# Expert loop of a mixture-of-experts encoder: token rows as the stationary operand, gate and up weights moving as high and low halves

## The reference, cut to what matters

```python
for e in range(N_EXPERTS):            # 32
    y = (jax.nn.silu(t @ e_gate[e]) * (t @ e_up[e])) @ e_down[e]
    out = out + combine[:, e:e + 1] * y
```

## Time and profile before

| | us |
|---|---|
| median of three runs (lowest, highest) | 893.04 (891.31, 894.35) |
| the profiled execution | 892.98 |
| its span | 891.0 |
| expert loop on PE, first transpose to last down matmul | 498.43 to 841.76 |

### The profile page before, as it was taken

The page is one execution under the profiler, slowest core; times in us unless marked ns, Lnnn a source line. Parts: engine busy times, 40 slices in busy tenths (PEclk is TensorE's granted clock), DMA queues, the critical chain, the costliest instruction groups (busy, mean ns, idle before and its releaser), DMA issues.

```text
span 891.0 us, 13079 instructions
## 1 busy us (share of the span) xinstructions
PE 771.9 (87%) x5022; PEld 641.3 (72%) x5022; DVE 373.1 (42%) x767; ACT 302.0 (34%) x539; POOL 329.7 (37%) x313
## 2 busy tenths in 40 slices
PE   3999999999977888999973599999999999999700
PEld 2788888866654554787873599999998899999600
DVE  5540000046768885412238233343333333333266
ACT  6211112145558887202220233333333333333222
POOL 2432256435556771501110123443433333442134
PEclk9999999979999999999995699999999999999955
DMA  8451112000010002426358189999999999996194
GB/s 273 108 151 48 47 48 71 1 0 1 2 48 0 1 1 76 137 69 219 113 172 300 38 258 335 351 349 351 348 349 350 347 342 347 350 352 231 40 370 195
DMA packets 111238, 160.21 MB, mean 180 GB/s; under 512 B 8304, under 2 KB 88656, under 8 KB 111072
## 3 DMA queue, kind: packets, MB, share of 16 engines
q1 hardware_dynamic: 104800, 142.78, 47.9%
q0 software_dynamic: 6400, 16.92, 5.9%
HBM read 144.99 MB, written 18.87 MB: 184 GB/s over the span
## 4 chain that ended last, share of the span: by engine, by line
PE 75%; DVE 9%; ACT 6%; DMA 4%; issue 3%; POOL 1%; SPq 1%; POOLq 0%; ACTq 0%; DVEq 0%
PE ps L768 26%; PE ps L583 6%; PE ps L585 6%; PE ps L584 6%; PE ps L788 3%; PE ps L787 3%; PE ps L792 3%; PE ps L623 3%; PE ps L759 2%; PE ps L648 2%; PE ps L707 2%; PE ps L709 2%; PE ps L708 2%; PE ps L664 2%; PE ps L670 2%
## 5 line engine op out<-in xcount | busy, mean ns | idle before, releaser
L768 PEld LDWEIGHTS ps<-xT,wg 128*128 128x128 f32 x1024 | 121.6, 195 | 5.9 <-ACT xT L1016 2.3
L768 PE MATMUL ps<-xT,wg 128*128 128x96 f32 x1024 | 121.4, 278 | 1.8 <-ACT xT L1016 1.8
L768 PE MATMUL ps<-xT,wu 128*128 128x96 f32 x1024 | 119.6, 275 | 0.0
L768 PEld LDWEIGHTS ps<-xT,wu 128*128 128x128 f32 x1024 | 116.9, 192 | 0.0
L1388 DVE TENSOR_TENSOR wdlo<-wd,wdhi 128x2048 fp32r<-128x2048 f32 x32 | 73.4, 2292 | 63.0 <-ACT wdhi L1036 63.0
L583 PE MATMUL ps<-hThi,whi 128*128 128x512 f32 x224 | 88.3, 394 | 4.2 <-DVE hTlo L1086 4.2
L585 PE MATMUL ps<-hThi,wlo 128*128 128x512 f32 x224 | 87.7, 392 | 0.0
L584 PE MATMUL ps<-hTlo,whi 128*128 128x512 f32 x224 | 87.7, 391 | 0.0
L1584 POOL COPY tokc<-tok 80x1 int32 (+1 forms) x32 | 54.1, 1689 | 42.7 <-DVE tok L1369 30.7
L1597 POOL COPY destc<-dest 80x1 int32 (+1 forms) x32 | 5.7, 178 | 166.7 <-DVE ysb L1380 166.7
L1536 POOL TENSOR_SCALAR pswa<-pswa,esum 128x384 f32<-128x384 f32 (+1 forms) x48 | 55.5, 1165 | 31.8 <-DVE esum L1173 31.4
(11 more groups left out here) (194 smaller groups left out, 1415.4 us busy)
## 6 DMA issues: line engine op xcount, KB each, us to landing
wg<-in_expert_w_gate SPq DMA_DIRECT2D x32, 1024.0 KB, 8.9
wu<-in_expert_w_up SPq DMA_DIRECT2D x32, 1024.0 KB, 12.7
wd<-in_expert_w_down SPq DMA_DIRECT2D x32, 1024.0 KB, 6.0
y<-expert_rows SPq DMA_DIRECT2D x16, 512.0 KB, 9.5
wraw<-in_w_in SPq DMA_DIRECT2D x14, 512.0 KB, 3.9
xin<-in_x SPq DMA_DIRECT2D x8, 512.0 KB, 5.6
xres<-in_x SPq DMA_DIRECT2D x16, 256.0 KB, 3.0
h_rows<-h SPq DMA_DIRECT2D x8, 512.0 KB, 2.7
```

The costliest lines, as they stand in the source:

```text
L768: mm = nc.tensor.matmul(ps[:, bank, f * COLS:(f + 1) * COLS], w[:, k, c0:c0 + P], xTu[:, k, :], start=(k == 0), stop=(k == KT - 1))
```

## The change

Gate and up are computed the way down already was. The gathered rows, transposed, are split into `xThi` and `xTlo` (80 columns, float32r) and are now the stationary operand. The gate and up weights move, 256 columns of gate and 256 of up side by side as 512, as a high part and a low part: 8 contraction pieces x 3 products = 24 matmuls of 512 columns per expert. The result has the tokens on the partitions, so the product `hx` (80x256) has to be transposed by PE (two pieces) before down.

The high parts live in `unit`, a ring of four 8 KB units per partition, three units per expert: two for the halves of gate and up, one for down. The low parts overwrite the loaded weights. ACT makes every high part (`half_high`, `down_high`), DVE every low part (`half_low`, `down_low`). The gate and up loads take 8 KB in one piece per partition ("(p k) f" in place of "(k p) f", with the h2 rows and the router weights permuted alike). The result rows leave PSUM in one ACT copy of 1024 columns. The index copies on POOL go. All loops over experts are written out in full.

The core of the diff:

```diff
+        unit = [at(f"unit{i}", [P, 2, 4 * DE], F32R, off) for i, off in enumerate((H + 56 * KB, H + 24 * KB, W + 56 * KB, V))]
+        def weight_unit(e, part):
+            return unit[(3 * e + (0, 1, 5)[part]) % 4]
+        def raw_half(w, e, a):
+            return w[e % RING][:, :, 4 * a:4 * a + 4, :].rearrange("p g k f -> p g (k f)")
 # SP
-                return (g_src.rearrange("(k p) f -> p k f", p=P), u_src.rearrange("(k p) f -> p k f", p=P),
+                return (g_src.rearrange("(p k) f -> p k f", p=P), u_src.rearrange("(p k) f -> p k f", p=P),
+                if e >= RING:
+                    sp.wait_ge(half_done, 2 * (e - RING) + 2)
...
+                if e >= RING:
+                    sp.wait_ge(down_done, e - RING + 1)
 # PE
+            def gate_up(e):
+                bank = ps[0:CAP, 2 + e % 2, :].rearrange("q (g f) -> q g f", g=2)
+                pe.wait_ge(xThi_done, e + 1)
...
+                for a in range(2):
+                    hi, lo = weight_unit(e, a), raw_half(wgulo, e, a)
+                    pe.wait_ge(ahi_done, 2 * e + a + 1)
+                    for k in range(4):   # xThi x hi
...
+                    for k in range(4):   # xTlo x hi
...
+                    pe.wait_ge(alo_done, 2 * e + a + 1)
+                    for k in range(4):   # xThi x lo
...
+                    mm.then_inc(half_done, 1)
+            def h_rows(e):
+                pe.wait_ge(h_made, e + 1)
+                for j in range(2):
+                    mm = nc.tensor.transpose(...)
+                mm.then_inc(htr_done, 1)
+            x_rows(0)
+            for e in range(N_EXP):
+                if e >= 1:
+                    h_rows(e - 1)
+                if e + 1 < N_EXP:
+                    x_rows(e + 1)
+                gate_up(e)
+                if e >= 1:
+                    down(e - 1)
+            h_rows(N_EXP - 1)
+            down(N_EXP - 1)
 # ACT
+            def half_high(e, a):
+                u = 3 * e + a
+                if a == 0:
+                    act.wait_ge(wgu_in[e % RING], 32 * (e // RING + 1))
+                if u >= 4:
+                    if a == 0:
+                        act.wait_ge(down_done, e - 1)
+                    else:
+                        act.wait_ge(half_done, 2 * (e - 1) + 1)
+                nc.scalar.copy(weight_unit(e, a)[:], raw_half(wgu, e, a)).then_inc(ahi_done, 1)
+            def down_high(e):
+                act.wait_ge(wd_in[e % RING], 16 * (e // RING + 1))
+                act.wait_ge(half_done, 2 * e + 2)
+                nc.scalar.copy(weight_unit(e, 2)[:], ...).then_inc(dhi_done, 1)
+            half_high(0, 0)            # ahead of the router's two Exp
...
+            half_high(0, 1)
+            x_high(0)
+            for e in range(N_EXP):
+                if e >= 1:
+                    h_high(e - 1)
+                if e + 1 < N_EXP:
+                    x_high(e + 1)
+                    half_high(e + 1, 0)
+                    half_high(e + 1, 1)
+                if e >= 2:
+                    rows_out(e - 2)
+                silu(e)
+                down_high(e)
 # DVE
+            for e in range(N_EXP):
+                if e >= 1:
+                    h_low(e - 1)
+                if e + 1 < N_EXP:
+                    x_low(e + 1)
+                    half_low(e + 1, 0)
+                    half_low(e + 1, 1)
+                gated(e)
+                down_low(e)
 # POOL: gather and scatter without the tokc and destc copies
-                gp.tensor_copy(tokc[u % 2][:], col).then_inc(idx_t, 1)
-                pool.wait_ge(idx_t, e + 1)
+                gp.indirect_dma_start(xg[e % 2][0:CAP, :], None, h2_d, bass.IndirectOffsetOnAxis(ap=tok[:, e:e + 1].bitcast(U32), axis=0),
```

More of the change, by code:

```diff
@@ L521, in _ @@
             sp.wait_ge(out_mm, 2 * TT)
[L522 to L526, removed]
+            for e in range(1, N_EXP):
+                fetch_expert(e)
             sp.dma_start(gbc[:], final_g.rearrange("(a d) -> a d", a=1).partition_broadcast(P)).then_inc(g_in, 16)
@@ L761, in ex_transposes, with x_rows @@
                 return mm
[L763 to L772, removed]
+            def x_rows(e):
+                pe.wait_ge(xg_in[e % 2], 16 * (e // 2 + 1))
+                if e >= 1:
+                    pe.wait_ge(xThi_done, e)
+                    pe.wait_ge(xTlo_done, e)
+                rows_transposed(xg[e % 2]).then_inc(etr_done, 1)
@@ L773, in down @@
                 for n in range(2):
                     for j in range(2):
-                        mm = nc.tensor.matmul(ps[0:CAP, b0 + n, :], hTu[:, j, 0:CAP], wd[u][:, j, n * 512:(n + 1) * 512],
-                                              start=(j == 0), stop=(j == 1))
-                return mm
[L779 to L788, removed]
+                        nc.tensor.matmul(ps[0:CAP, b0 + n, :], hThi_e[:, j, :], hi[:, j, n * 512:(n + 1) * 512], start=(j == 0), stop=False)
@@ L811, in down_of @@
[L811 to L823, removed]
+                        nc.tensor.matmul(ps[0:CAP, b0 + n, :], hTlo_e[:, j, :], hi[:, j, n * 512:(n + 1) * 512], start=False, stop=False)
@@ new lines, in down @@
+                    if n == 0:
+                        pe.wait_ge(dlo_done, e + 1)
+                    for j in range(2):
+                        mm = nc.tensor.matmul(ps[0:CAP, b0 + n, :], hThi_e[:, j, :], wdlo[e % RING][:, j, n * 512:(n + 1) * 512],
+                                              start=False, stop=(j == 1))
+                mm.then_inc(down_done, 1)
+            pe.wait_ge(hx_zero, 1)
+            x_rows(0)
[7 more added lines that the diff above has]
+                    down(e - 1)
@@ new lines, in _, with v_gate_up, v_down @@
+            h_rows(N_EXP - 1)
+            down(N_EXP - 1)
+            def v_gate_up(xTu):
+                for f in range(4):
+                    c0 = (f % 2) * P
+                    for k in range(KT):
+                        mm = nc.tensor.matmul(ps[:, 2, f * COLS:(f + 1) * COLS], wgu[0][:, f // 2, k, c0:c0 + P], xTu[:, k, :],
+                                              start=(k == 0), stop=(k == KT - 1))
+                return mm
+            def v_down(hTu):
+                for n in range(2):
+                    for j in range(2):
+                        mm = nc.tensor.matmul(ps[0:CAP, 4 + n, :], hTu[:, j, 0:CAP], wd[0][:, j, n * 512:(n + 1) * 512],
+                                              start=(j == 0), stop=(j == 1))
+                return mm
@@ L1013, in _ @@
             nc.scalar.activation(rs[:, 9, 0:TT], rs[:, 8, 0:TT], ACT.Exp).then_inc(r_exp, 1)
[L1015 to L1024, removed]
-                act.wait_ge(etr_done, e + 1)
-                if not first or u >= 2:
-                    act.wait_ge(gu_done, e - 1)
-                xT_copy(xT[u % 2]).then_inc(xT_done, 1)
-                if not first or u >= 2:
-                    y_low(it, u)
-                act.wait_ge(wd_in[u], it * 16 + 16)
-                if not first or u >= 2:
-                    act.wait_ge(down_done, e - 1)
-                elif u == 0:
-                    act.wait_ge(tok_done, 2)
-                nc.scalar.copy(wdhi[u % 2][:], wd[u][:]).then_inc(wdhi_done, 1)
-                act.wait_ge(gu_done, e + 1)
-                silu(sg[u % 2], 2 + u % 2).then_inc(silu_done, 1)
@@ L1040, in y_low @@
-            def y_low(it, u):
-                e = it * RING + u
-                par = u % 2
-                act.wait_ge(down_done, e - 1)
-                if not (isinstance(it, int) and it == 0):
-                    act.wait_ge(y_put[par], put_count(it, u - 2))
-                nc.scalar.copy(ysb[par][:, 0:512], ps[0:CAP, 4 + 2 * par, :]).then_inc(y_a, 1)
-            for u in range(RING):
-                expert(0, u)
-            with act.Fori(1, N_EXP // RING) as it:
-                for u in range(RING):
-                    expert(it, u)
@@ L1054, in _, with x_high, h_high @@
-            y_low(N_EXP // RING, 0)
-            y_low(N_EXP // RING, 1)
+            def x_high(e):
+                act.wait_ge(etr_done, e + 1)
+                if e >= 2:
+                    act.wait_ge(half_done, 2 * (e - 2) + 2)
+                nc.scalar.copy(xThi[e % 2][:].rearrange("p (b c) q -> p b c q", b=2),
+                               ps[:, 0:2, 0:4 * COLS].rearrange("p b (c q) -> p b c q", c=4)[:, :, :, 0:CAP]).then_inc(xThi_done, 1)
+            def h_high(e):
+                act.wait_ge(htr_done, e + 1)
+                if e >= 1:
+                    act.wait_ge(down_done, e)
+                nc.scalar.copy(hThi_e[:], ps[:, 2 + e % 2, 0:2 * COLS].rearrange("p (j q) -> p j q", j=2)[:, :, 0:CAP]).then_inc(hThi_done, 1)
@@ new lines, in silu, with rows_out @@
+            def silu(e):
+                act.wait_ge(half_done, 2 * e + 2)
+                if e >= 1:
+                    act.wait_ge(h_made, e)
+                nc.scalar.activation(sg[:], ps[0:CAP, 2 + e % 2, 0:DE], ACT.Silu).then_inc(silu_done, 1)
+            def rows_out(e):
```

(48 more changed lines are left out.)

211 lines of the change are left out of this document (102 added, 109 removed).

## The result

The changed kernel takes 1288.37 us (median of four runs, 1285.79 to 1289.01) against 892.82 for the kernel before, measured beside it: a ratio of 1.4425 with a 95% interval of 1.4393 to 1.4457. The forecast was 1172 with a range up to 1235. The direction was right; the size was missed by 116 us, and the range by 53.

A forecast was written before the change was run, and what follows sets the result against it. The prediction took PE to bound the kernel before, at 10.55 us per expert. With waits in series, a period became 19.85 us and the loop 281.0 us longer: 892.98 + 281.0 - 1.1 - 0.7 = 1172 us, range 1105 to 1235.

The forecast's parts named there:

- What bounds the kernel before: Expert loop before the change: PE alone bounds it, 10.55 us per expert; loads at 348 GB/s are the near second limit.
- The wait of half_high and its 7.1 us: After each down, PE stands idle 7.1 us until ACT and DVE have made the next expert's weights and the product.
- Nothing else is late there: PE's work after that wait (h_rows, x_rows, gate_up, down): no further wait, so nothing added to the period.
- off the path, as POOL waits: Gathers: only the first index copy and its wait count, -1.1 us once; the others add nothing.
- The low clock: Each PE burst starts at 1.2 GHz, rising 5.25 us into gate_up: transposes 1.54 us, gate_up 8.0 us.
- The sum: Period 7.1 + 0.4 + 1.54 + 8.0 + 2.78 = 19.85 us; 30 periods 595.5 us; whole loop 624.3 against 343.3.
- Head and end: Loop parts outside the 30 periods: 24.1 us for iterations 0 and 1, 4.7 us for the last expert.
- rival 2: Loop: the clock never comes back inside a burst; period 24.5 us, 1324 us in all; chance 0.09.
- The start and end terms: Outside the loop: -1.1 us at the first gather, -0.7 us after the loop, 0 for the second normalisation.
- 1: Rival for the loop: the clock stays full; period 16.3 us, 1062 us in all; chance 0.07.
- Rival 3: Loop: half_high(e+1, 0) runs under gate_up(e); period 9.2 us, 853 us, or 893 with loads at 348 GB/s; chance 0.04.
- the 884 us: Loop of Rival 3 held by the skill's 358 GB/s HBM limit: 10.25 us per expert, 884 us in all.

The follow-up runs named there:

- e8_before_8kb: The kernel before the change with only the 8 KB pieces for gate and up (h2 rows and router weights permuted alike): 894.39 us, ratio 0.9996.
- e1_count: The changed kernel with one edit: half_high(e, 0) waits for down(e-3) instead of down(e-2). 1203.77 us, ratio 1.3496.
- e2_pool_order: The changed kernel with one edit: on GpSimd the scatter of e-2 in place of e-1 follows the gather of e+2. 1133.01 us, ratio 1.2670.
- e7_warm: e2_pool_order with 80 matmuls of 128 columns per expert, never read, put into PE's idle time before h_rows: 1067.05 us, ratio 1.1928.
- e3_both: The changed kernel with the edits of both e1_count and e2_pool_order: 873.24 us, ratio 0.9770.
- e4_both_1kb: e3_both with gate and up loads back in 1 KB pieces, router weights and second normalisation in their old order: 890.86 us, ratio 0.9963.

## Why the prediction missed: point by point

- **What bounds the kernel before:** right, by e8_before_8kb.
- **The wait of half_high and its 7.1 us:** right. From T, the end of the last down matmul at 713.2, PE is idle for 6.9 us until h_rows at 720.08; taking the count away in e1_count removed this wait.
- **The failed step: "Nothing else is late there", with the gathers counted as "off the path, as POOL waits".** I followed what stands behind half_high(e+1, 0) on ACT, DVE and PE, but not on GpSimd. rows_out(e-2) is one of those instructions; scatter(e-2) waits for it; and behind that scatter, in GpSimd's list, stands the gather of e+2, whose rows PE transposes right after h_rows(e). The prediction put this wait at nothing; it measured 5.6 us per expert. Moving the scatter one place back in e2_pool_order removed it and took 155 us off.
- **Its length was to be had from the trace before.** There a scatter keeps GpSimd for 0.94 us, and a gather of the loop lands 6.6 to 7.5 us after its issue (600 to 811 us). With rows_out ending at T + 4.8 and 0.3 between the two, the rows come near T + 13, against a PE that wants them at T + 7.5. They came at T + 13.1 (726.23), by other parts: scatter at 718.68 for 1.8 us, gather at 720.80, landing 5.4 us later.
- **The low clock:** its mechanism is shown, with an oversized term. In the changed kernel PE begins transposes at 726.23 and gate_up at 727.5, and the clock is back at 730.1, after 2.7 us of gate_up, where before it was 5.25:

```profile
726.00:730.00 4.00, 3.77 (x14) 2.85 (x15) 0.82 (x1) 0.69 (x1) 0.00 (x0) 0.50 0.00 0
730.00:734.00 4.00, 4.00 (x18) 2.51 (x17) 0.00 (x0) 0.00 (x0) 0.00 (x0) 0.98 0.02 4
```

  Transposes, gate and up take 8.1 us there (726.23 to 734.3) and not 9.54. One event of the trace before was too little to give this number: the rise comes 2.3 to 3 us into gate_up in most experts of the changed kernel, and 1.6 to 4.9 us into it in e2_pool_order. The estimate of 0.43 us for a matmul of 512 columns at 1.2 GHz is confirmed: four take 1.71 us from start to start (e1_count, 724.15 to 725.86).
- **The sum.** Per expert +5.6 for the gather and -1.4 for the clock make 24.05 in place of 19.85; 28 of the 30 periods measured 23.9 in the mean. The first (19.2) and the last (17.0) lack the wait for the gather. So the 30 periods took 706.3 us and not 595.5, which is 111 of the 116 us missed. Head and end were right (23.9 for 24.1, 4.6 for 4.7). Two slips of the sum are too small to matter: its parts give 19.82 and not 19.85, and rival 2 comes to 1323 and not 1324.
- **The start and end terms** are the other 5 us. The first transposes stand at 501.77 where 497.3 was forecast, in part because the first gather kept GpSimd for 2.62 us and not 1.15; after the loop 49.5 us were left, and not 48.5. The second normalisation's strided read went from 1.28 us to 2.22 us each; e8_before_8kb, which has it, shows no cost clear of the noise.
- **Rivals:** 1 is out, as the granted clock is 0.50 from 726 to 730, and e7_warm is what it would have given. 2 is out, as the clock is at 0.98 from 730 to 734; that its 1324 us lie nearer to the measured 1288 than the forecast is chance. Rival 3 described a kernel that waits rightly; e3_both is that kernel, at 873 us between its 853 and 893.
- **The bandwidth figures.** The page "DMA: Bandwidth & Descriptors" of the Trainium skill gives 358 GB/s from HBM per core (specifications). Under its measured bandwidths the same page says that this is a core's part with both cores of a pair streaming. Here one core ran alone and e3_both moved 371 GB/s, so the 884 us drawn from that figure were no floor. The specifications also name 512 B as the least transfer for line rate. With 1 KB pieces and the DMA share full, e4_both_1kb moved 347 GB/s, and with 8 KB pieces e3_both moved 371, so above 512 B the length of a piece still counted here.

## What to carry to other kernels

Where a wait comes late, follow every engine's list behind it to its next hand-over, the engine that issues DMAs above all: a store that waits for a late result holds back the next load that stands behind it, though the two have nothing to do with each other. In a ring whose order differs from the order of use, work out the count of each wait from the slot's last reader; one count too many looks safe and put 7 us in series with nearly each of 32 experts. Two late waits can hide each other's worth: mended one at a time they gave 85 and 155 us, and together 415. A small gain from mending one wait does not clear it; look at whether another wait has grown in its place, as the one for the gather did here, from 5.6 to 11.0 us, when the loads moved beside it.

## What the hardware showed that I had not expected

- A gather of 80 rows of 4 KB landed 5.4 us after its issue when three loads of 1 MB had been issued some 7 us ahead of it, 11.3 us with the three issued within 1.1 us after it (9.8 to 11.9 over the experts of e1_count), and 5.8 us once those were held back. In e1_count this contention alone cost 127 us.
- An indirect DMA kept GpSimd for 0.91 to 0.98 us (once 1.15) when no large DVE instruction was under way at its start, and for longer when one of DVE's low parts was (`wgulo` or `wdlo`, two inputs in SBUF, 2.29 us): then it ended 0.79 to 0.85 us after that low part, in every expert's gather and scatter of the changed kernel's loop and of its mended forms. Three lines of the changed kernel show it, with the gather at 720.80 above (until 723.10, 0.83 us after the `wdlo`):

```profile
504.06 0.95 POOL L1655 DMA_INDIRECT xg<-h_rows,tok  x1 [3.34 <-PE ps L768]
719.98 2.29 DVE L1440 TENSOR_TENSOR wdlo<-wd,unit 128x2048 fp32r<-128x2048 f32 x1
1224.55 0.93 POOL L1660 DMA_INDIRECT expert_rows<-ysb,dest  x1 [2.20 <-ACT ysb L1094]
```

  The form of the instruction, with its indices in a column of a wide tile, is the same at 504.06 and at 720.80, so the form is not the cause. That GpSimd waits for DVE here is read from these times; no run moves the two apart. In the changed kernel it adds some 2.2 us to the late scatter and gather (1.81 and 2.30 for 0.93 and 0.95).
- Matmuls kept the clock up without being of use: 80 small ones per expert made e7_warm 66 us faster than the same kernel without them.
